# Two-layer mixer encoder on one core: one-time steps inside layer 0, and two projection groups with high and low part in one matmul

## The chip, the cores and the metric

The kernel runs on one core of a Trainium2 chip. The metric is the device time in microseconds (us) of one execution. The kernel before takes 1415.18 us, the median of three runs (1415.05 to 1416.42).

## The reference, cut to what matters

An encoder of two layers works on 256 tokens of width 1024, with a second input `mem` of 256 rows. All values are float32.

```python
for i in range(DEPTH):                       # DEPTH = 2
    h = rms_norm(x, mix_norm_g[i])
    proj = h @ w_in[i]      # attention q, k, v | ssm z | ssm xBC | ssm dt | memory q | gates
    y_da  = diff_attention(q, k, v, lam, ...)                 # 8 heads, alibi slopes
    y_ssm = mamba2_bidir(z, xbc, dt, conv_w, conv_b, ...)     # conv of 5 taps over xbc, chunked scan, both ways
    y_xa  = mem_cross_attention(xa_q, rms_norm(mem, mem_norm_g[i]), w_mem_kv[i])
    merged = g0 * (y_da @ wb_da) + g1 * (y_ssm @ wb_ssm) + g2 * (y_xa @ wb_xa)
    x = x + merged @ w_out[i]
    x = x + swiglu(rms_norm(x, ffn_norm_g[i]))
return rms_norm(x, final_norm_g)
```

`lam` is a scalar of each layer, made from exponentials of four short parameter vectors.

## The kernel before, in words

**High and low parts.** Every large product is made from float32 values split in two: a high part (the value cast to the matmul type fp32r) and a low part (what is left). For a weight W and an activation A the kernel adds W_high x A_high, W_high x A_low and W_low x A_high in PSUM. ScalarE casts the weights (`wH`, L990, `split_h`); VectorE (L1382) or, for some units, GpSimd (L1317) subtracts and writes `wL` (`split_l`).

**Units.** The weights of a layer come as 220 units of 128x1024 floats (512 KB): two K tiles of 128 rows by 512 columns. A ring of four slots holds raw, high and low part. Units are grouped (`layer_groups`); a group of four units fills one of two PSUM pairs (`PS[0]`, `PS[1]`, 1024 columns each), which alternate by the parity of the group. A group of layout T computes the transposed product: in a unit, for each of four column blocks and two K tiles, a matmul of 256 columns with A_high and one with A_low (16), and then eight with W_low: 24 matmuls. Layout N has 12 matmuls of 512 columns. Layout C (most of the FFN) streams `hHL`, where high and low activation lie side by side, as one operand of 512 columns: eight of those and eight of 256 columns; the two halves of the result are added later. C needs twice the PSUM for the same output columns, and takes it from the side banks `S`.

**The order of a layer.** The groups run mk0, mk1, mv0, mv1 (keys and values of `mem`, units 0 to 15), dt (16, 17), xbc4 (18 to 21), xq0 (22 to 25), xbc5 (26 to 29), xq1, xbc0, q0, k0, v0, xbc1, q1, k1, v1 (62 to 65), xbc2, z3, z0 and so on to br, out, ffn and down.

**A plan written out by hand** (`layer_plan`) says after which unit each engine does each side step: `put(u, engine, step, i)`. Each engine walks the units in order (`each_step`): at unit u TensorE does the matmuls of u and then its steps of u; ScalarE does first the cast of unit u+3 and then its steps of u, in the order in which they were put; VectorE does first the subtraction of unit u+3 (where GpSimd does not have it) and then its steps; the SyncE queue issues the load of unit u+3. The cast of u+3 waits until TensorE has used the slot, that is until unit u-1 is done. `pool_splits` gives GpSimd the odd units from 8 on, but none from unit 26 to the gates of branch 1.

**Around units 18 to 28.** TensorE does `dt_turn` after unit 19 and `dt_sums` after unit 25; VectorE does `dt_in` at 20, `dt_u` at 21 (L1660 to L1665), `dt_out` at 23 and the first four conv steps at 22 to 25 (L1646, each four instructions); ScalarE does `dt_exp` at 21, `dt_ln` at 23, and evacuates xbc4 at 22 (L1018 and four of L1022) and xq0 at 26 (L1002). `psum_free` of a pair is raised by whoever evacuated it, and TensorE waits for it at the first unit of the group that uses the pair next.

**The start.** Ahead of unit 0 TensorE transposes `mem` (`mem_turn`, four parts, two of them before unit 0 and two ahead of units 1 and 2), ScalarE scales it and casts units 0 to 2. Then, still ahead of its first planned step, ScalarE squares `mem` (L1043, twice, into row sums), takes the root (L1049), issues the load of x, and takes the exponentials for `lam` (L1263, L1265); VectorE makes the reciprocal, the two diagonal tiles `mdiag` (L1417) and the sums for `lam`. Only after this come the casts of unit 3 and later. `mem_row` on TensorE, after unit 3, broadcasts `mdiag` with two small matmuls. `norm_square` to `norm_scale` (steps 2 to 5) normalise x for `norm_turn` after units 9 to 12. `par_turn` (TensorE, after unit 4) and `params` (VectorE, step 5) bring the parameters (L1398 to L1411).

**The end.** The last `down` group finishes token half 0 before half 1. VectorE adds (L1461) and multiplies by the gain (L1464), ScalarE squares and takes the root (L1279, L1281), and then VectorE (L1823, L1826) and, for the first 512 columns of half 1, ScalarE (L1284) scale; one store for each half follows.

Of the kernel before, what the change touches and what calls it, by code (L numbers as in the profile page):

```python
# [33 lines left out]
ALU = mybir.AluOpType  # L34
AX = mybir.AxisListType

P = 128
# [38 lines left out]
def layer_groups():  # L76
# [11 lines left out]
    return g  # L88


GROUPS = layer_groups()
# [4 lines left out]
assert UNITS % RING == 0 and NGROUPS % 2 == 0  # L96
# [11 lines left out]
def layer_plan():  # L108
# [10 lines left out]
    for g, (kind, b, units, _) in enumerate(GROUPS):  # L119
        if kind == "mk":  # L120
            put(FIRST_UNIT[g] + units + 1, "dve", "mk", g)
        if kind in ("mv", "xq", "q", "k", "v", "xbc", "z", "gate0", "gate1", "gate2"):
# [43 lines left out]
    for h in range(HEADS):  # L166
# [6 lines left out]
        put(u + 4, "pe", "da_turn", h)  # L173
        put(u + 5, "act", "da_copy", h)
        put(u + 6, "pe", "da_values", h)
        put(u + 7, "act", "da_head", h)
# [29 lines left out]
    for i in range(4 * SG):  # L206
# [5 lines left out]
        put(x[i] + 6, "pe", "diag", i)  # L212
# [67 lines left out]
PAR_LOADS, ROW_LOADS = 6, 7  # L280


def build(nc, x, mem, mix_norm_g, w_in, lq1, lk1, lq2, lk2, subln_g, conv_w, conv_b, dt_bias, A_log, D_skip,
# [3 lines left out]
    with ctx:  # L287
# [71 lines left out]
        def conv_tile(n):  # L359
# [12 lines left out]
        sg1 = [sg, scr[:, 0:1024]]  # L372
        hid = scr[:, 0:512]
# [48 lines left out]
            "turned", "h", "ready", "sq", "sum", "std", "diag", "row"))  # L422
        sp_pace, pe_pace = sem("sp_pace"), sem("pe_pace")
# [40 lines left out]
        def unit_source(lay, g, c):  # L464
# [11 lines left out]
            if kind.startswith("br"):  # L476
# [3 lines left out]
                   "gate1": GATE0 + D, "gate2": GATE0 + 2 * D}[kind]  # L480
            return cols(w_in_v, lay, k, col + UC * b)
# [13 lines left out]
        def used_after(lay, g):  # L495

            return lay * (NGROUPS // 2) + g // 2 + 2

        def wait_full(eng, lay, g):

            u = FIRST_UNIT[g] + GROUPS[g][2] - 1
            eng.wait_ge(unit_used[u % RING], use(lay, u) + 2)

        def wait_evacuated(eng, lay, kind, b):
            g = GI[kind, b]
            eng.wait_ge(psum_free[g % 2], used_after(lay, g))
# [26 lines left out]
        def _(sp):  # L533
# [6 lines left out]
            def load(lay, u):  # L540
# [17 lines left out]
                else:  # L558

                    src = unit_source(lay + u // UNITS, g, c)  # L560
                    sp.dma_start(raw[:, slot], src).then_inc(raw_in[slot], 32)
# [57 lines left out]
            sp.dma_start(gB, final_norm_g.partition_broadcast(P)).then_inc(fin_in, 16)  # L619
            sp.wait_ge(fin_second, 1)  # L620
# [5 lines left out]
        def _(pe):  # L626
# [29 lines left out]
            for b in range(2):  # L656
                mem_turn(b)
# [37 lines left out]
            def unit(lay, u, g, c):  # L695
                kind, b, units, layout = GROUPS[g]
                slot, pair = u % RING, g % 2
# [4 lines left out]
                if c == 0 and kind != "outb":  # L702
                    pe.wait_ge(psum_free[pair], lay * (NGROUPS // 2) + g // 2 + 1)
# [3 lines left out]
                if lay == 0 and kind == "mk" and b == 0 and c in (1, 2):  # L707
                    mem_turn(c + 1)
                first_unit, last_unit = c == 0 and kind != "outb", c == units - 1 and kind != "out"
                if layout == "T":  # L710
                    for m in range(4):
                        for kk in range(UT):
# [5 lines left out]
                            mm(o, w_h, aL_[:, k, :], False, False)  # L718
                    pe.wait_ge(l_done[slot], use(lay, u) + 2)
                    for m in range(4):  # L720
                        for kk in range(UT):
                            w_l = wL[:, slot, kk, P * m:P * (m + 1)]
                            ins = mm(dst[:, T * m:T * (m + 1)], w_l, aH_[:, a0 + UT * c + kk, :], False,
                                     last_unit and kk == UT - 1)
                elif layout == "C":
# [245 lines left out]
        def _(act):  # L971
# [21 lines left out]
            def evac(lay, g):  # L993
                kind, b = GROUPS[g][:2]
                pair = g % 2
# [80 lines left out]
            def step(lay, kind, i):  # L1076
                if kind == "evac":
# [26 lines left out]
                elif kind == "hid_corr":  # L1104
                    g = GI["ffn", i]
                    pair = g % 2
# [83 lines left out]
                elif kind == "dt_copy":  # L1190
                    g = GI["dt", 0]
                    wait_full(act, lay, g)
                    nc.scalar.copy(dtT, PS[g % 2][0:64, 0:T]).then_inc(psum_free[g % 2], 1)
# [64 lines left out]
            for t in range(NT):  # L1258
                mem_square(t)
            mem_root()  # L1260
            act.dma_start(xN, x.rearrange("b (t p) d -> p (b t) d", p=P)).then_inc(x_in, 16)
            act.wait_ge(row_in, 16 * ROW_LOADS)
# [588 lines left out]
```

## Time and profile before

| what | value |
|---|---|
| median of three runs | 1415.18 us (1415.05 to 1416.42) |
| the profiled execution, its own time | 1415.59 us |
| its span | 1413.9 us, 22066 instructions |
| TensorE matmul busy | 1393.2 us (99%), 8199 instructions |
| weight loads busy | 1222.2 us (86%) |
| VectorE, ScalarE, GpSimd busy | 923.6 (65%), 884.6 (63%), 322.9 us (23%) |
| DMA | 253.85 MB, mean 180 GB/s |
| mean granted TensorE clock | 0.997 of full speed |

The span runs from the first instruction to the last; the profiled execution's own time is 1.7 us longer than its span and 0.41 us longer than the median. Matmuls are pipelined: what one costs is read from start to start, not from its duration.

### The profile page before, as it was taken

To read this page: it belongs to the slowest core of one execution; us is meant where nothing else is said; L and a number is where in the kernel's file an instruction comes from. 1 tells how busy PE (TensorE), PEld (TensorE's weight loads), DVE (VectorE), ACT (ScalarE), POOL (GpSimd) and SP (SyncE) were. 2 spreads that over 40 slices of the span, in tenths; PEclk is the share of its full clock that TensorE was granted. 3 is DMA by queue.
4 is the path that set the end of the run, shared out by engine and by line. 5 is a ranking of instruction groups with operands and counts; after the bars stand their busy time and mean duration, and the time that the engine had idled before them with its cause. 6 is when DMAs were issued, how large, how long until landed. Compare 5 with 4: busy or idle time off the path is not lost.

```text
span 1413.9 us, 22066 instructions
## 1 busy us (share of the span) xinstructions
PE 1393.2 (99%) x8199; PEld 1222.2 (86%) x8215; DVE 923.6 (65%) x1246; ACT 884.6 (63%) x1428; POOL 322.9 (23%) x161
## 2 busy tenths in 40 slices
PE   6999999999999999999999999999999999999998
PEld 6899898888888889888899998988888888888886
DVE  5567565898998545554453775668989874555532
ACT  6567567886855546555445765878777563555543
POOL 0310000010023444444414000000110244444442
PEclk9999999999999999999999999999999999999999
DMA  7565445566765555656556554465767545566663
GB/s 258 170 195 167 133 135 164 142 194 217 204 189 171 197 179 176 196 181 229 188 184 179 155 163 136 134 179 142 215 200 223 188 165 191 167 192 181 193 193 119
DMA packets 158181, 253.85 MB, mean 180 GB/s; under 512 B 12681, under 2 KB 59899, under 8 KB 157819
## 3 DMA queue, kind: packets, MB, share of 16 engines
q1 hardware_dynamic: 157347, 250.73, 57.6%
q10 hardware_dynamic: 728, 1.71, 0.3%
q8 instruction: 65, 1.06, 0.3%
q14 instruction: 41, 0.34, 0.1%
HBM read 250.18 MB, written 2.23 MB: 179 GB/s over the span
## 4 chain that ended last, share of the span: by engine, by line
PE 88%; DVE 4%; ACT 3%; DVEq 2%; issue 1%; DMA 1%; ACTq 0%; SPq 0%
PE PS L635 71%; PE S L635 14%; DVE wL L1382 1%; ACT wH L990 1%; PE S L642 1%; ACT scr L1148 1%; DMA w_raw<-in_w_in_dram 1%; DVE actLf L1646 1%; PE S L959 0%; PE S L894 0%; DVEq L1717 0%; DVEq L1648 0%; DMA regA<-in_mem_dram 0%; PE S L865 0%; DVE regA L1718 0%
## 5 line engine op out<-in xcount | busy, mean ns | idle before, releaser
L990 ACT CAST wH<-w_raw 128x1024 fp32r<-128x1024 f32 x440 | 457.9, 1043 | 461.0 <-PE PS L635 323.5
L1382 DVE TENSOR_TENSOR wL<-w_raw,wH 128x1024 fp32r<-128x1024 f32 (+1 forms) x328 | 415.5, 1271 | 337.0 <-ACT wH L990 318.4
L1317 POOL TENSOR_TENSOR wL<-w_raw,wH 128x1024 fp32r<-128x1024 f32 (+1 forms) x112 | 270.8, 2418 | 417.3 <-ACT wH L990 417.3
L635 PE MATMUL PS<-hHL,wH 128*128 128x256 f32 (+2 forms) x2016 | 314.8, 303 | 0.0
L635 PEld LDWEIGHTS PS<-hHL,wH 128*128 128x128 f32 (+1 forms) x2016 | 266.4, 190 | 10.9 <-issue 2.6
L635 PE MATMUL PS<-wH,actH 128*128 128x512 f32 x560 | 223.1, 398 | 0.0
L635 PE MATMUL PS<-wH,actL 128*128 128x512 f32 x560 | 218.4, 390 | 0.0
L635 PE MATMUL PS<-wH,hHL 128*128 128x512 f32 x768 | 200.7, 403 | 0.0
L635 PE MATMUL PS<-hHL,wL 128*128 128x256 f32 (+1 forms) x1168 | 172.0, 283 | 0.0
L635 PEld LDWEIGHTS PS<-wH,hHL 128*128 128x128 f32 x768 | 140.1, 188 | 33.2 <-issue 6.5
L635 PEld LDWEIGHTS PS<-hHL,wL 128*128 128x128 f32 (+1 forms) x1168 | 158.4, 190 | 6.2
L635 PE MATMUL PS<-wL,actH 128*128 128x512 f32 x560 | 150.9, 390 | 0.0
L635 PEld LDWEIGHTS PS<-wH,actL 128*128 128x128 f32 x560 | 105.3, 188 | 22.3 <-issue 1.4
L635 PEld LDWEIGHTS PS<-wH,actH 128*128 128x128 f32 x560 | 105.2, 188 | 22.3 <-issue 1.4
L635 PEld LDWEIGHTS PS<-wL,actH 128*128 128x128 f32 x560 | 105.1, 188 | 22.3
L635 PE MATMUL PS<-wL,hHL 128*128 128x512 f32 x384 | 103.2, 390 | 0.0
L635 PE MATMUL S<-hHL,wH 128*128 128x512 f32 x320 | 85.9, 390 | 0.0
L635 PEld LDWEIGHTS PS<-wL,hHL 128*128 128x128 f32 x384 | 72.1, 188 | 15.9
L1344 POOL TENSOR_TENSOR scr<-actHf,dts 128x512 f32<-128x512 f32 x16 | 20.6, 1286 | 271.0 <-PE S L865 207.2
L1333 POOL TENSOR_TENSOR regA<-actHf,dts 128x512 f32<-128x512 f32 x8 | 10.1, 1266 | 269.9 <-ACTq L1189 228.2
L635 PEld LDWEIGHTS S<-hHL,wH 128*128 128x128 f32 x320 | 60.1, 188 | 13.5
L1646 DVE SCALAR_TENSOR_TENSOR actLf<-scr,lp,actLf 128x256 f32<-128x256 f32 x128 | 59.5, 506 | 4.7 <-issue 0.4
(256 smaller groups left out, 1578.3 us busy)
## 6 DMA issues: line engine op xcount, KB each, us to landing
w_raw<-in_w_in_dram SPq DMA_DIRECT2D x192, 512.0 KB
w_raw<-in_w_ffn_in_dram SPq DMA_DIRECT2D x176, 256.0 KB
w_raw<-in_w_branch_dram SPq DMA_DIRECT2D x64, 512.0 KB
w_raw<-in_w_ffn_out_dram SPq DMA_DIRECT2D x44, 512.0 KB
w_raw<-in_w_mem_kv_dram SPq DMA_DIRECT2D x32, 512.0 KB
regA<-cs_rows SPq DMA_DIRECT2D x64, 256.0 KB, 5.2
w_raw<-in_w_out_dram SPq DMA_DIRECT2D x16, 512.0 KB
regA<-in_mem_dram SPq DMA_DIRECT2D x4, 256.0 KB, 5.8
```

The source lines that it names most:

```text
L635: return nc.tensor.matmul(o, l, r, start=first, stop=last, skip_group_check=True)
L642: ins = nc.tensor.transpose(dst[:, at:at + P], src(t, k), ident[:, :])
L990: nc.scalar.copy(wH[:, slot].rearrange("p k c -> p (k c)")[:, q], raw[:, slot].rearrange("p k c -> p (k c)")[:, q]).then_inc(h_done[slot], 1)
L1148: ins = nc.scalar.activation(sc[b][:, T * q:T * (q + 1)], S[q // 2][:, T * (q % 2):T * (q % 2 + 1)], ACT.Exp, bias=nmx[b][:, q:q + 1], sca ...
L1317: nc.gpsimd.tensor_tensor(wL[:, slot].rearrange("p k c -> p (k c)")[:, q], raw[:, slot].rearrange("p k c -> p (k c)")[:, q], wH[:, slot].r ...
L1333: nc.gpsimd.tensor_tensor(v3(xw[i % 2], HPG), v3(xsN[g][:, 1 - c, :], HPG), wgt[:, q:q + HPG].unsqueeze(2).broadcast_to([P, HPG, DH]), ALU ...
L1344: nc.gpsimd.tensor_tensor(v3(xsd[i % 2], HPG), v3(xsN[g][:, c, :], HPG), dgain[:, SH * c + HPG * g:SH * c + HPG * (g + 1)].unsqueeze(2) .b ...
L1382: v.tensor_tensor(wL[:, slot].rearrange("p k c -> p (k c)")[:, q], raw[:, slot].rearrange("p k c -> p (k c)")[:, q], wH[:, slot].rearrange ...
L1646: ins = v.scalar_tensor_tensor(tile[:, j, :], cin[:, j, k:k + T], p_cw[:, q:q + 1], tile[:, j, :], ALU.mult, ALU.add)
```

## The change

1. A new layout W for two groups, xbc4 and xq0. A unit holds four K tiles by 256 columns instead of two by 512; its matmuls stream `hHL` (512 columns) for W_high. Two units fill one PSUM pair (a *fill*), so a W group takes two fills, and the parity of pairs counts fills. Each fill is evacuated by a copy of the low halves on ScalarE (`wide_corr`) and an addition on VectorE (`wide_sum`), which frees the pair. The evacuations of xbc4 (step 22) and xq0 (step 26) on ScalarE go; for xbc4, the middle tap is made from SBUF in `conv_mid`.
2. The squares and root of `mem`, the load of x and the steps for `lam` move from before the first planned step to steps 1 to 6 of layer 0; `params`, and the four steps of the norm of x, move by one to three units. Of the `mem_turn` parts, one is before unit 0 and three lie inside units 0 to 2, after the second column block.
3. Three moves of side steps: `da_turn` to `da_head` of the last head by one unit, the first `cb` from unit 68 to 61, `diag` 11 from unit 108 to 109.
4. At the end each half is scaled right after its root, half by VectorE and half by ScalarE (half 1: 384 columns on ScalarE).

```diff
+WIDE = [("xbc", 4), ("xq", 0)]
+FILLS = [2 if x[3] == "W" else 1 for x in GROUPS]
+FIRST_FILL = [sum(FILLS[:i]) for i in range(NGROUPS)]
+PAIR = [n % 2 for n in FIRST_FILL]
...
+        if (kind, b) in WIDE:
+            for half in range(2):
+                n = 2 * WIDE.index((kind, b)) + half
+                put(FIRST_UNIT[g] + 2 * half + 2, "act", "wide_corr", n)
+                put(FIRST_UNIT[g] + 2 * half + 2, "dve", "wide_sum", n)
+                if kind == "xbc":
+                    put(FIRST_UNIT[g] + 2 * half + 3, "act", "conv_mid", n)
...
-    put(5, "dve", "params")
+    put(7, "dve", "params")
     put(6, "sp", "mem_keep")
+    put(1, "act", "mem_stats")
+    put(2, "dve", "mem_stats")
+    put(4, "dve", "lam_sum")
+    put(5, "act", "lam_exp")
+    put(6, "dve", "lam_out")
     put(3, "pe", "mem_row")
     put(4, "dve", "mem_row")
-    put(2, "act", "norm_square")
-    put(3, "dve", "norm_sum")
-    put(4, "act", "norm_root")
-    put(5, "dve", "norm_scale")
+    put(4, "act", "norm_square")
+    put(5, "dve", "norm_sum")
+    put(6, "act", "norm_root")
+    put(8, "dve", "norm_scale")
...
+        last = h == HEADS - 1
+        put(u + 4 + last, "pe", "da_turn", h)
+        put(u + 5 + last, "act", "da_copy", h)
+        put(u + 6 + last, "pe", "da_values", h)
+        put(u + 7 + last, "act", "da_head", h)
...
-        u = x[4 * g] + (-1, -5, -5, -6)[g]
+        u = x[4 * g] + (-8, -5, -5, -6)[g]
         put(u, "pe", "cb", g)
         put(u + 1, "act", "cb_rows", g)
...
-        put(x[i] + 6, "pe", "diag", i)
+        put(x[i] + (7 if i == 11 else 6), "pe", "diag", i)
...
+                at = col + UC * b + T * (c // 2)
+                return w_in_v[lay, :, 4 * (c % 2):4 * (c % 2) + 4, at:at + T]
...
-            for b in range(2):
-                mem_turn(b)
+            mem_turn(0)
...
-                if c == 0 and kind != "outb":
-                    pe.wait_ge(psum_free[pair], lay * (NGROUPS // 2) + g // 2 + 1)
+                if c == 0 and kind != "outb" or layout == "W" and c == 2:
+                    pe.wait_ge(psum_free[pair], lay * (LAYER_FILLS // 2) + fill // 2 + 1)
...
+                        if lay == 0 and kind == "mk" and b == 0 and c < 3 and m == 1:
+                            mem_turn(c + 1)
...
+                elif layout == "W":
+
+                    at = 4 * (c % 2)
...
+                    for m in range(2):
+                        for kk in range(4):
+                            mm(dst[:, 2 * T * m:2 * T * (m + 1)], w_h[:, kk, P * m:P * (m + 1)], hHL[:, at + kk, :, :],
+                               c % 2 == 0 and kk == 0, False)
+                    pe.wait_ge(l_done[slot], use(lay, u) + 2)
+                    for m in range(2):
+                        for kk in range(4):
+                            ins = mm(dst[:, 2 * T * m:2 * T * m + T], w_l[:, kk, P * m:P * (m + 1)], hH[:, at + kk, :],
+                                     False, c % 2 == 1 and kk == 3)
...
+                if kind == "wide_corr":
+                    g, half = GI[WIDE[i // 2]], i % 2
+                    pair = (PAIR[g] + half) % 2
+                    wait_full(act, lay, g, half)
+                    nc.scalar.copy(v3(corr[pair], 2), halves(PS[pair][:, :])[:, :, 1, :]).then_inc(wide_corr, 1)
+                elif kind == "conv_mid":
+                    b, half = WIDE[i // 2][1], i % 2
+                    act.wait_ge(wide_done, 2 * len(WIDE) * lay + i + 1)
+                    for j in range(2 * half, 2 * half + 2):
...
+                elif kind == "mem_stats":
+                    if lay == 0:
+                        act.dma_start(xN, x.rearrange("b (t p) d -> p (b t) d", p=P)).then_inc(x_in, 16)
+                        for t in range(NT):
+                            mem_square(t)
+                        mem_root()
+                elif kind == "lam_exp":
+                    if lay == 0:
+                        act.wait_ge(row_in, 16 * ROW_LOADS)
+                        nc.scalar.activation(rows3[:, :, 64:128], rows3[:, :, 64:128], ACT.Exp)
+                        act.wait_ge(lam_sum, 1)
+                        nc.scalar.activation(lam4, lam4, ACT.Exp)
+                        act.drain().then_inc(lam_exp, 1)
...
-            act.wait_ge(fin_rstd, NT)
-            nc.scalar.activation(fin[:, 1, 0:UC], fin[:, 1, 0:UC], ACT.Copy, scale=xr[:, 1:2]).then_inc(fin_first, 1)
-            act.wait_ge(fin_first, 1)
+                act.wait_ge(fin_rstd, t + 1)
+                q = slice(UC, D) if t == 0 else slice(0, FIN_ACT)
+                nc.scalar.activation(fin[:, t, q], fin[:, t, q], ACT.Copy, scale=xr[:, t:t + 1]).then_inc(fin_first, 1)
+            act.wait_ge(fin_first, 2)
...
+                    dve.wait_ge(wide_corr, 2 * len(WIDE) * lay + i + 1)
+                    v.tensor_tensor(dst, halves(PS[pair][:, :])[:, :, 0, :], v3(corr[pair], 2), ALU.add
+                                    ).then_inc(psum_free[pair], 1)
+                    dve.drain().then_inc(wide_done, 1)
+                elif kind == "mem_stats":
+                    if lay == 0:
+                        dve.wait_ge(mem_std, 1)
+                        v.reciprocal(mr, mr)
+                        dve.drain()
+                        mem_factors()
...
-                    if i % 4 == 0:
+                    if ("xbc", b) in WIDE:
+                        dve.wait_ge(conv_mid, 2 * lay + i % 4 // 2 + 1)
+                    elif i % 4 == 0:
                         wait_evacuated(dve, lay, "xbc", b)
```

## Rows read from the trace of the kernel before

**Rows 1.** Page, part 4: the chain that ended last, by engine

```profile
PE 88%; DVE 4%; ACT 3%; DVEq 2%; issue 1%; DMA 1%; ACTq 0%; SPq 0%
```

**Rows 2.** Waits of TensorE: who for whom, us in total, times, longest

```profile
PE PS L635 <- ACT wH L990: 5.1, 1, 5.1
...
PE S L865 <- DVEq L1623: 0.8, 2, 0.4
PE S L635 <- ACT scr L1148: 0.7, 2, 0.4
```

**Rows 3.** Timeline, TensorE: start, duration; units 24 and 25 (T), dt_sums, unit 26

```profile
86.20 2.08 PE L635 MATMUL PS<-hHL,wH 128*128 128x256 f32 x16
...
89.08 2.08 PE L635 MATMUL PS<-hHL,wH 128*128 128x256 f32 x16
...
91.96 0.20 PE L635 MATMUL S<-aH,upR 128*128 128x64 f32 x1
...
92.58 2.13 PE L635 MATMUL PS<-hHL,wH 128*128 128x256 f32 x16
```

**Rows 4.** Timeline, TensorE, the first matmuls of two units of layout C

```profile
569.21 1.09 PE L635 MATMUL PS<-hHL,wH 128*128 128x512 f32 x4
...
572.00 1.09 PE L635 MATMUL PS<-hHL,wH 128*128 128x512 f32 x4
```

**Rows 5.** The chain in order of time: start, us; all of unit 3

```profile
24.75 5.11 PE PS L635 x24
```

**Rows 6.** Timeline, ScalarE and VectorE, the steps ahead of the first planned one

```profile
17.51 1.06 ACT L1043 ACTIVATE regA<-regA 128x1024 f32<-128x1024 f32 x1
...
21.04 0.30 ACT L1049 ACTIVATE small<-small 128x2 f32<-128x2 f32 x1
...
21.62 0.48 DVE L1417 TENSOR_SCALAR regB<-ident,small 128x128 f32<-128x128 f32 x2
...
23.56 2.94 ACT L990 CAST wH<-w_raw 128x1024 fp32r<-128x1024 f32 x3
```

**Rows 7.** Timeline, TensorE, the first matmul of unit 5

```profile
33.26 0.36 PE L635 MATMUL PS<-actH,wH 128*128 128x256 f32 x1
```

**Rows 8.** DMA view of 0 to 40 us, one figure per us

```profile
GB/s 0 21 215 236 207 236 367 393 401 379 371 371 265 151 87 33 18 162 344 410 408 307 393 385 184 25 18 207 309 322 193 303 420 449 401 367 367 340 326 209
```

**Rows 9.** Windows: stretch, busy times of the engines, granted TensorE clock, DMA

```profile
24.70:27.00 2.30, 2.25 (x10) 2.28 (x11) 2.30 (x3) 1.82 (x3) 0.00 (x0) 0.50 0.06 24
```

**Rows 10.** Timeline, ScalarE, VectorE and GpSimd, steps 21 to 24 of layer 0

```profile
80.18 0.31 ACT L1197 ACTIVATE scr<-scr 128x128 f32<-128x128 f32 x1
...
82.56 1.93 ACT L1022 ACTIVATE regA<-PS,lp 128x256 f32<-128x256 f32 x4
...
82.10 2.27 DVE L1665 TENSOR_TENSOR scr<-scr,dts 128x128 f32<-128x128 f32 x1
...
91.10 1.23 DVE L1382 TENSOR_TENSOR wL<-w_raw,wH 128x1024 fp32r<-128x1024 f32 x1
92.24 1.83 DVE L1646 SCALAR_TENSOR_TENSOR regA<-scr,lp,regA 128x256 f32<-128x256 f32 x4
...
81.82 2.40 POOL L1317 TENSOR_TENSOR wL<-w_raw,wH 128x1024 fp32r<-128x1024 f32 x1 [3.82 <-ACT wH L990]
```

**Rows 11.** Groups of 560 to 640 us: xcount, busy us, mean ns, idle before

```profile
L1108 ACT COPY scr<-PS 128x512 f32<-128x512 f32 x7 | 4.1, 580 | 0.0
...
L1550 DVE TENSOR_TENSOR scr<-PS,scr 128x512 f32<-128x512 f32 x7 | 4.8, 692 | 13.5 <-ACT scr L1109 13.5
```

**Rows 12.** Timeline, TensorE, end of unit 108 and diag 11

```profile
390.33 1.07 PE L635 MATMUL PS<-wL,hHL 128*128 128x512 f32 x4
391.71 1.10 PE L635 MATMUL S<-actHf,regA 128*128 128x64 f32 x8 [0.31 <-DVEq L1728]
```

**Rows 13.** Timeline, the end: VectorE scales half 0; the last store is issued

```profile
1408.73 0.75 DVE L1826 TENSOR_SCALAR regB<-regB,small 128x1024 f32<-128x1024 f32 x1
...
1410.37 0.35 ACTq L1287 DMA_DIRECT2D out_dram<-regB  x1
```

More of the change, by code:

```diff
@@ L87, in layer_groups @@
     g += [("down", nb, FT // UT, "N") for nb in range(2)]
-    return g
+    return [(kind, b, n, "W" if (kind, b) in WIDE else layout) for kind, b, n, layout in g]
+WIDE = [("xbc", 4), ("xq", 0)]
 GROUPS = layer_groups()
@@ L493, in past_end, with used_after, wait_full @@
             return lay == DEPTH - 1 and u >= UNITS
[L495 to L501, printed above, removed]
+        def used_after(lay, fill):
+            return lay * (LAYER_FILLS // 2) + fill // 2 + 2
+        def wait_full(eng, lay, g, half=1):
+            u = FIRST_UNIT[g] + (GROUPS[g][2] - 1 if half else 1)
             eng.wait_ge(unit_used[u % RING], use(lay, u) + 2)
@@ L505, in wait_evacuated @@
             g = GI[kind, b]
-            eng.wait_ge(psum_free[g % 2], used_after(lay, g))
+            fill = FIRST_FILL[g] + FILLS[g] - 1
+            eng.wait_ge(psum_free[fill % 2], used_after(lay, fill))
         def each_step(engine, unit_fn, evac_fn, step_fn):
@@ L696, in unit @@
                 kind, b, units, layout = GROUPS[g]
-                slot, pair = u % RING, g % 2
+                fill = FIRST_FILL[g] + (c // 2 if layout == "W" else 0)
+                slot, pair = u % RING, fill % 2
                 if kind == "ffn" and b in (1, 2) and c == 0:
@@ L1192, in step @@
                     wait_full(act, lay, g)
[L1193 removed]
+                    nc.scalar.copy(dtT, PS[PAIR[g]][0:64, 0:T]).then_inc(psum_free[PAIR[g]], 1)
                     act.drain().then_inc(dt_copied, 1)
@@ L1493, in step @@
                     params(lay)
+                elif kind == "wide_sum":
+                    (what, b), half = WIDE[i // 2], i % 2
+                    g = GI[what, b]
+                    pair = (PAIR[g] + half) % 2
+                    q = slice(2 * half, 2 * half + 2)
+                    if what == "xq":
+                        if lay == 0 and b == 0:
+                            dve.wait_ge(mem_stored, 16)
+                        dst = xqT[:, 4 * b:4 * b + 4, :][:, q]
+                    else:
+                        dst = cin[:, q, 2:2 + T]
+                    dve.wait_ge(wide_corr, 2 * len(WIDE) * lay + i + 1)
[8 more added lines that the diff above has]
+                        mem_factors()
+                elif kind == "lam_sum":
+                    if lay == 0:
+                        dve.wait_ge(row_in, 16 * ROW_LOADS)
+                        lam = scr[:, 2048:2560].rearrange("p (a q c) -> p a q c", a=2, q=2)
+                        v.tensor_tensor(v3(scr[:, 4096:4352], 2), lam[:, :, 0, :], lam[:, :, 1, :], ALU.mult)
+                        dve.drain()
+                        v.tensor_reduce(lam4, scr[:, 4096:4352].rearrange("p (a c) -> p a c", a=4), AX.X, ALU.add)
+                        dve.drain().then_inc(lam_sum, 1)
+                elif kind == "lam_out":
+                    if lay == 0:
+                        v.memset(cin[:, :, 0:2], 0.0)
+                        v.memset(cin[:, :, 2 + T:4 + T], 0.0)
+                        dve.wait_ge(lam_exp, 1)
+                        v.tensor_tensor(nlam2, lam4[:, 2:4], lam4[:, 0:2], ALU.subtract)
+                        dve.drain()
+                        for n in range(DEPTH):
+                            v.tensor_scalar(nlam2[:, n:n + 1], nlam2[:, n:n + 1], -lambda_init(n), None, ALU.add)
+                        dve.drain()
                 elif kind == "norm_sum":
```

86 lines of the change are left out of this document (34 added, 52 removed).

## The prediction

> **What bounds the kernel now.** The chain that ended last comes first: 88% of it is TensorE [rows 1], so apart from the start and the end only two things count, the distance of matmuls from start to start and the waits of TensorE. The waits view lists nearly all of the second kind: one of 5.1 us in the start, and five short ones in the body, of which two pairs are shown [rows 2] and the fifth is 0.31 us [rows 12]. The timeline gives the first kind: a unit of layout T takes 89.08 - 86.20 = 2.88 us [rows 3], one of layout C, with the same products, 572.00 - 569.21 = 2.79 us [rows 4]. VectorE and ScalarE are 65% and 63% busy over the span, but this mean says little: around unit 24 VectorE has no idle time at all, and that is where the change gives it more work.
>
> **Layout W, what it saves.** W has the matmuls of C (eight of 512 columns, eight of 256). The saving is 2.88 - 2.79 = 0.09 us a unit, for 8 units in each of two layers: 0.7 us a layer, 1.4 us in all. From below it could be nothing; more than this no row supports. Its loads are rows of 1 KB where T has 2 KB; the FFN loads have 1 KB too and layout C still goes at its pace, so I count nothing; were a load late, the ring of four slots (some 8 us) covers it.
>
> **Layout W, what it adds.** Per fill, ScalarE gets a copy of 128x512 (0.58 us) and VectorE an addition of 128x512 (0.69 us), both read from the same pair of operations in the FFN [rows 11]. ScalarE loses two copies of 128x1024 for four of these and comes out even. VectorE gets four additions, 2.8 us a layer, and the pair is now freed by the last of a chain: matmuls, copy, addition. Behind each addition, on VectorE's queue, stand the conv step and the later `split_l`; in front of it stands all that VectorE is late with. So each must be walked. With TensorE 0.09 us a unit quicker, unit 24 would start at 85.66 and unit 26 at 91.86 (now 92.58 [rows 3], less 8 x 0.09).
> - `wide_sum` 0 (step 20): VectorE is idle there; nothing waits.
> - Step 21: ScalarE now does `conv_mid` 0 (half of the 1.93 us of four activations) ahead of `dt_exp`. It begins 0.3 us earlier, so `dt_exp` ends at 81.1 instead of 80.49 [rows 10]. `dt_u` follows; its multiplication, a 128x128 operation, took 2.27 us, since it ended with GpSimd's subtraction (81.82 + 2.40 = 84.22; the multiplication ended at 84.37 [rows 10]). The same collision comes 0.4 us later: GpSimd to 84.6, `dt_u` to 84.75.
> - `wide_sum` 1 (step 22): 84.85 to 85.55. It frees the pair of unit 24 (85.66): just in time, 0 to 0.4 us late. I take 0.
> - `conv` 0: 85.6 to 87.5; `split_l` 26 to 88.65; `dt_out` (1.6) to 90.3; `conv` 1 (1.9) to 92.2. Now the same point is 91.10 [rows 10].
> - Step 24: `split_l` 27 (1.14 from 91.10 to 92.24 [rows 10]) to 93.3, and only then `wide_sum` 2 to 94.0. It frees the pair that xbc5, unit 26, needs at 91.86. TensorE waits 2.15 us. Even without any delay in the steps before, 91.10 + 1.14 + 0.69 = 92.93 would be 1.1 us late.
> - `wide_sum` 3 (step 26) ends near 101; its pair is wanted by unit 30, near 106. Nothing.
>
> A small SBUF operation that finishes with GpSimd's, as in rows 10, is also what a page describes. The Trainium skill, SBUF — State Buffer, "SBUF: two separate sides", says that VectorE's operations with two SBUF inputs and GpSimd's take one pair of ports whole, one after the other. By that rule `wide_sum`, with one input in PSUM, is never held up. The trace agrees: in the FFN the like addition takes 692 ns in the mean, although GpSimd subtracts there too [rows 11].
>
> So W costs 2.15 - 0.70 = +1.45 us a layer, **+2.9 us** in both; ends: -1.4 (no wait) and +4.0 (2.7 us of wait).
>
> **The start.** TensorE waits 5.1 us before unit 3, from 19.6 to 24.75, because ScalarE reaches the cast of unit 3 only at 23.56 [rows 6], and unit 3 then takes 5.11 us [rows 5] instead of 2.88: the granted clock is 0.50 there [rows 9], 1.2 GHz. Unit 5 starts at 33.26 [rows 7]. After the change the cast of unit 3 comes at once, and unit 3 runs at full clock from about 20.1 to 23.0 (the later `mem_turn` parts cost ScalarE 1.3 us, which this leaves out of no sum, since a later wait hides it). But `mem_row` stays after unit 3 and needs `mdiag`, and this moved:
> - ScalarE, step 1: the cast of unit 4 must have its load. The loads of 4 and 5 were issued at 12; little moved from 14 to 17 [rows 8]; about 0.9 MB had come by 20. Estimate: cast from 20.1 to 21.2.
> - The load of x issues here, behind that wait, 1 us or so later than now; `norm_square` wants it at 28, when it lands.
> - Squares, table load, root: 17.51 to 21.34, 3.83 us [rows 6], now to 25.0.
> - Step 2: the cast of unit 5 (2.94 / 3 = 0.98 [rows 6]) to 26.0; VectorE subtracts (1.2) to 27.25, and only then makes reciprocal and tiles (0.8, as from 21.34 to 22.10 [rows 6]): 28.1.
>
> TensorE stands from 23.0 to 28.15: 5.1 us again. The wait has only changed its name. Unit 4 starts at 28.6. After an idle time of the same length I take the same half clock: 5.1 to 5.2 us, then `par_turn`, and unit 5 at 34.15: **+0.9 us**. Ends: -1.5 if the clock stays up, +2 if it comes back a unit later or if the next point fails. Steps 4 to 8 on VectorE: `params` and `norm_scale` (8) end near 47.9 by my walk, with one more wait for GpSimd; `norm_turn` after unit 9 comes at 48.1. Cover: 0.2 us. `lam` itself has room to unit 48.
>
> The Trainium skill, TensorE: Matmul & The Clock Gate, "What's actually happening", says that the monitor of the clock runs freely, so that the moment of a change differs from run to run. By that rule the same gap may in some executions cost no half clock, and the start would come out at -1.5. The one trace shown has a single gap of this length and it did fall, and the three runs lie within 1.4 us, so this is a rival and not the forecast.
>
> **Three moved steps.** `da_turn` of head 7 and the first `cb` wait in both layers (waits of 0.8 and 0.7 in all [rows 2]), `diag` 11 in layer 0 (0.31 [rows 12]): 1.8 us. From start to start they cost more: the last matmul before `diag` 11 starts at 390.33 + 3 x 0.227 = 391.01, the next would be due at 391.24, and it starts at 391.71: 0.47 us. The other four, read so, are 0.52 to 0.57; sum 2.65, and with the unit behind it 2.7. Ends: 0 (each finds a wait in its new place) and -2.8. At 61 bank 0 has been free since `da_exp` 59, and `xs_turn` in it comes a unit later; `da_turn` 7 has a whole unit for what was 0.4 us late; bank 2 is wanted again only at 81. I take **-2.7 us**.
>
> **The end.** Now VectorE scales all of half 0 from 1408.73 to 1409.48 [rows 13], and the reciprocal of half 1 stands behind it. Half 0 would be done before half 1 arrives (delay of half 1: 0.1 us at most), the reciprocal comes 0.5 us earlier, and the last store issues at 1409.9 instead of 1410.37 [rows 13]. The two stores, now 0.9 us apart, no longer share the DMA engines; I add 0.5 us for that, a guess from the 3.5 us from that issue to the end. **-1.0 us**; ends -0.3 and -1.4.
>
> **Sum:** +2.9 + 0.9 - 2.7 - 1.0 = +0.1 us on 1415.59, which is 1415.7; the median of the runs is 0.41 lower, so 1415.3. This measurement can tell about 0.2%, 2.8 us, from no change.
>
> **Rivals.**
> - *VectorE keeps up* and TensorE does not wait at unit 26. For it: if the multiplication in `dt_u` gets in before GpSimd, the walk is 1.7 us shorter and the wait 0.4. Against: now, without any addition, VectorE is already too late by 1.1. W then gives -1.4, the total is -4.2: 1411. Chance 0.22. With the next one besides, 1408.7: 0.05.
> - *The clock stays up* over the gap before `mem_row`: -2.3, total -2.2, 1413. 0.16.
> - *Slower:* the clock falls in the new gaps ahead of unit 26. It needs 2.2 us of idle to be enough; then unit 26 costs 2.2 us more (5.11 against 2.88), twice: 1415.3 + 4.4 = 1419.7. Against: no gap in the body shown is that long, and in the start it took 5.1. 0.08.
> - *VectorE is late for `norm_turn`*, by a further subtraction of GpSimd (2.4), or moved steps wait again: +2 to +3, 1417.5 to 1418.5. 0.09.
> - That the change does not do what it says is part of the forecast: the start is not shortened.
>
> **Numbers.** The forecast's own case has 0.40, and its own range is 1413.5 to 1417.3. The range of 8 in 10 takes in most of *keeps up* and of *late for norm_turn*: 1410.4 to 1418.5. Faster: 0.22 + 0.05 and 0.06 from the low ends of the others, 0.33. Slower: 0.08, half of 0.09, and 0.06 for a wait that I don't see, 0.19. Within: 0.48.
>
> **What would show it.** Waits of TensorE: `psum_free` from the new addition ahead of unit 26, near 2 us in both layers (right), or none (the first rival); a wait of `mem_row` near 5 us in place of that before unit 3, and the granted clock of unit 4; none left for L865, the first `cb` and `diag` 11; W units at 2.79 us; the last store some 3.4 us before the end. If unit 5 starts before 32.5, my start is wrong; if xbc5 starts within 0.7 us of xq0's end and `dt_sums`, my walk of VectorE is.

## The result, and the profile after

| | median, us | executions | lowest to highest |
|---|---|---|---|
| before, beside it | 1415.47 | 12 | 1413.89 to 1416.42 |
| after | 1419.38 | 12 | 1416.83 to 1421.12 |

The ratio is 1.0026, with a 95% interval of 1.0019 to 1.0033: slower by 3.9 us. The forecast was 1415.3 with a range up to 1418.5; the measured median lies 4.1 us above the first and 0.9 us above the second. The profiled execution of after took 1420.75 us, its span is 1419.0 against 1413.9: 5.1 us more.

The waits of TensorE (for whom, us in total, times, longest) answer to [rows 2]:

```profile
PE S L663 <- DVEq L1479: 4.4, 1, 4.4
PE PS L663 <- DVE regA L1576: 4.1, 2, 2.1
PE PS L663 <- ACT wH L1032: 3.0, 1, 3.0
...
PE S L907 <- DVEq L1732: 0.3, 1, 0.3
```

The first is the wait of `mem_row`, in place of the 5.1 us before unit 3. The second is new: twice 2.07 us, ahead of unit 26 in each layer, released by `wide_sum` 2 (L1576 adds). The third lies ahead of unit 0, at 7.70 us, where TensorE waits for the first cast; the trace before waits there for loads of `mem` instead (1.25 and 2.17 us). The waits of `da_turn` 7, `cb` 0 and `diag` 11 are gone. So far this is the forecast. The last row isn't: it is a wait of 0.26 us for VectorE ahead of `da_turn` 4 in layer 1 (949.33 us), where the trace before has none. The chain by engine has changed too [rows 1]:

```profile
PE 95%; DVE 2%; ACT 1%; DVEq 1%; issue 1%; DMA 0%; SPq 0%; ACTq 0%
```

This share can't tell where the time went: it is 95% too in the trace of a1 below, whose span is 8.0 us shorter, and 85% in that of c1, 3.4 us shorter. The starts of units can. The timeline of TensorE around unit 26 of layer 0 (start, duration) answers to [rows 3]:

```profile
81.51 2.00 PE L663 MATMUL PS<-hHL,wH 128*128 128x512 f32 x8
...
84.30 2.00 PE L663 MATMUL PS<-hHL,wH 128*128 128x512 f32 x8
...
89.93 2.00 PE L663 MATMUL PS<-hHL,wH 128*128 128x512 f32 x8
...
93.23 0.28 PE L663 MATMUL S<-aL,onesR 128*128 128x128 f32 x1
95.57 3.68 PE L663 MATMUL PS<-hHL,wH 128*128 128x256 f32 x16 [2.07 <-DVE regA L1576]
...
100.04 2.08 PE L663 MATMUL PS<-hHL,wH 128*128 128x256 f32 x16
```

A unit of W takes 84.30 - 81.51 = 2.79 us, as layout C does. The 16 matmuls of unit 26, behind the wait, take 3.68 us where those of unit 27 take 2.08; the unit as a whole takes 100.04 - 95.57 = 4.47 us instead of some 2.9. The windows say why (the last columns: granted clock, share of the DMA engines, GB/s):

```profile
93.30:95.50 2.20, 0.20 (x2) 0.06 (x1) 2.13 (x3) 1.21 (x2) 0.00 (x0) 1.00 0.05 20
95.50:97.00 1.50, 1.43 (x7) 1.43 (x8) 1.29 (x4) 0.00 (x0) 0.00 (x0) 0.56 0.57 66
97.00:98.00 1.00, 1.00 (x6) 1.00 (x6) 0.92 (x3) 0.00 (x0) 0.00 (x0) 0.50 0.94 365
98.00:99.00 1.00, 1.00 (x6) 1.00 (x6) 1.00 (x2) 0.00 (x0) 0.00 (x0) 0.50 0.17 61
99.00:100.00 1.00, 1.00 (x10) 1.00 (x9) 0.93 (x3) 0.00 (x0) 0.00 (x0) 0.95 0.18 14
```

The clock is 1.00 while TensorE stands, and falls to 0.50 (1.2 GHz) as unit 26 begins: 6 matmuls a us instead of 10 or 11. It is back near 99.1. Layer 1 shows the same, with the same 2.07 us of wait:

```profile
789.52 0.28 PE L663 MATMUL S<-aL,onesR 128*128 128x128 f32 x1
791.86 1.55 PE L663 MATMUL PS<-hHL,wH 128*128 128x256 f32 x6 [2.07 <-DVE regA L1576]
```

One such fall, 3.4 us at half the clock (here from about 95.7 to 99.1), lowers the mean clock of an execution by 3.4 x 0.5 / 1419 = 0.0012 (an estimate from these rows), so two make it 0.994 where it would be 0.997. Not every execution falls so. The mean clock of the twelve, beside their times:

```
0.994:  1419.36 1419.39 1419.43 1419.90 1420.72 1420.75 1421.12
0.996:  1417.18 1418.93
0.997:  1416.83 1417.26 1417.49
```

Seven have 0.994, as two falls give; the four lowest are near 1417, at 0.996 and 0.997; the one of 1418.93 could have one fall. Only one execution has a full trace here; that the low ones kept the clock at unit 26 is read from these two columns alone. The trace of a1, which has no gap at unit 26, has 0.996 too, so 0.996 doesn't tell one fall from none. The experiment d1 below shows by itself that the loss hangs on the idle time.

VectorE's queue shows why `wide_sum` 2 is late. Steps 21 to 24 of layer 0, which answer to the VectorE rows of [rows 10]:

```profile
84.25 1.95 DVE L1776 TENSOR_TENSOR scr<-scr,dts 128x128 f32<-128x128 f32 x1
86.28 0.69 DVE L1576 TENSOR_TENSOR scr<-PS,scr 128x512 f32<-128x512 f32 x1
87.12 1.83 DVE L1757 SCALAR_TENSOR_TENSOR regA<-scr,lp,regA 128x256 f32<-128x256 f32 x4
...
91.79 1.83 DVE L1757 SCALAR_TENSOR_TENSOR regA<-scr,lp,regA 128x256 f32<-128x256 f32 x4
93.69 1.23 DVE L1443 TENSOR_TENSOR wL<-w_raw,wH 128x1024 fp32r<-128x1024 f32 x1
94.83 0.68 DVE L1576 TENSOR_TENSOR regA<-PS,scr 128x512 f32<-128x512 f32 x1
```

The addition of 0.68 us is done at 95.51. In the queue it stands behind conv 1 (91.79) and the subtraction for unit 27 (93.69), which nobody waits for yet.

The start, on TensorE: end of unit 3, `mem_row`, unit 4, unit 5.

```profile
22.89 1.12 PE L663 MATMUL PS<-actH,wL 128*128 128x256 f32 x8
28.43 1.19 PE L663 MATMUL S<-regB,onesR 128*128 128x128 f32 x4 [4.43 <-DVEq L1479]
29.28 0.56 PE L663 MATMUL PS<-actH,wH 128*128 128x256 f32 x1
...
34.66 0.36 PE L663 MATMUL PS<-actH,wH 128*128 128x256 f32 x1
```

Unit 4 takes 5.38 us, nearly all of it at half clock, and unit 5 comes 1.40 us later than in [rows 7]. Not all of this comes from the wait: unit 0 took 6.10 us here (7.70 to 13.80) and 5.17 before (8.01 to 13.18). The end: half 0 stored early, half 1 last.

```profile
1413.33 0.36 SPq L649 DMA_DIRECT2D out_dram<-regB  x1
...
1415.94 0.35 ACTq L1348 DMA_DIRECT2D out_dram<-regB  x1
```

The last issue lies 3.06 us before the end of the span; before it was 1413.9 - 1410.37 = 3.53 us [rows 13].

The bookkeeping of the two profiled executions, by the starts of units: start +1.4; W -0.55 in each layer; wait +2.14 in each (89.08 to 92.58 before, 89.93 to 95.57 now); half clock +1.54 in each; moved steps about -1.2 in layer 0 and -0.35 in layer 1; end -1.0. Sum 1.4 - 1.1 + 4.3 + 3.1 - 1.6 - 1.0 = +5.1. The -0.35 holds a loss of 0.37 at `da_turn` 4, the row of 0.3 above. The waits views of all six kernels below with layout W on show it, and none with W off does, so it belongs to W.

### The profile page after: what moved, and what is told of

It reads as the page before. It is cut to its first block, busy times and chain, and to the rows that moved or that the text cites. A ratio compares the mean times of both kernels' runs of the same rounds, so it can differ in the third digit from the quotient of the medians.

```text
span 1419.0 us, 21836 instructions
## 1 busy us (share of the span) xinstructions
PE 1396.9 (98%) x8071; PEld 1219.8 (86%) x8087; DVE 928.5 (65%) x1254; ACT 884.8 (62%) x1433; POOL 322.8 (23%) x161
## 3 DMA queue, kind: packets, MB, share of 16 engines
q10 hardware_dynamic: 728, 1.71, 0.3%
## 4 chain that ended last, share of the span: by engine, by line
PE 95%; DVE 2%; ACT 1%; DVEq 1%; issue 1%; DMA 0%; SPq 0%; ACTq 0%
PE PS L663 76%; PE S L663 16%; PE S L670 1%; PE S L907 1%; PE S L936 1%; PE S L1001 1%; ACT wH L1032 0%; DVE wL L1443 0%; DMA w_raw<-in_w_mem_kv_dram 0%; DVE regA L1757 0%; DVE scr L1776 0%; PE S L876 0%; PE S L927 0%; DVEq L1759 0%; DVEq L1578 0%
## 5 line engine op out<-in xcount | busy, mean ns | idle before, releaser
L663 PEld LDWEIGHTS PS<-hHL,wH 128*128 128x128 f32 (+1 forms) x1888 | 260.2, 192 | 19.4 <-DVE regA L1576 4.4
L1757 DVE SCALAR_TENSOR_TENSOR actLf<-scr,lp,actLf 128x256 f32<-128x256 f32 x128 | 56.3, 481 | 5.0 <-issue 0.9
```

Source lines behind the costliest of these rows:

```text
L663: return nc.tensor.matmul(o, l, r, start=first, stop=last, skip_group_check=True)
L1757: ins = v.scalar_tensor_tensor(tile[:, j, :], cin[:, j, k:k + T], p_cw[:, q:q + 1], tile[:, j, :], ALU.mult, ALU.add)
```

## The experiments

Each kernel was measured beside the kernel before on the same chip. Its medians there were 1415.20 us (a1 to a4), 1415.22 (b4, b1, c1, c2) and 1414.94 (d1, b3). Unless it is said otherwise a kernel is the one after with the edit shown, and "after" and "before" are the two kernels of this document. Beside the kernel after it was 1415.47, so a time set straight against 1419.38 holds up to 0.5 us of difference between chips; each ratio is taken against the kernel before beside it and free of this. Brackets hold its 95% interval.

**a1: layout W off.**

```diff
-WIDE = [("xbc", 4), ("xq", 0)]
+WIDE = []
```

> The changed kernel with both W groups back in layout T; start, moved steps and end as changed. Theory (the wait for wide_sum 2 ahead of unit 26, and the half clock after it, make the change slow): both waits of 2.1 us go, and the clock stays up at unit 26. Start +1.4, moved steps -1.6, end -1.0 remain: 1.2 us faster than before, within 0.5 us of that in every execution, and no second drop of the clock. Rival (the start is what costs, and W is near neutral): 3 to 4 us slower than before, as the changed kernel is.

Measured: 1413.15 us (1412.73 to 1414.94, 11 executions), ratio 0.9988 [0.9979, 0.9996]. No wait ahead of unit 26 and no fall of the clock there. Layout W costs 1419.38 - 1413.15 = 6.2 us (6.0 if each is taken against the kernel before beside it), and the rest of the change gains 2.05, more than the 1.2 expected. By the starts of units between this trace and that of after, W costs -0.54 + 2.14 + 1.54 around unit 26 in each layer, 6.3 us.

**a2: the conv steps of xbc4 two units later.**

```diff
-            put(u + q, "dve", "conv", 4 * n + q)
+            put(u + q + (2 if b == 4 else 0), "dve", "conv", 4 * n + q)
```

> The changed kernel with the four conv steps of xbc4 on VectorE two units later (24 to 27), so that wide_sum 2 is not behind two of them. Theory (VectorE's queue order is the cause): wide_sum 2 ends near 93.4, at the time at which unit 26 is due; the wait shrinks from 2.1 us to under 0.3 us in both layers, unit 26 runs at full clock, W then saves its 0.09 us a unit: 2.3 us faster than before, and 5 to 7 us faster than an execution of the changed kernel with two drops. Rival (the addition's place in the chain copy, addition, free is too late in itself): a wait of 1 us or more stays, and the time is near 1415.

Measured: 1415.98 us (1414.85 to 1417.89), ratio 1.0005 [0.9996, 1.0014]. The wait at unit 26 is gone and the clock stays up there, 3.4 us less than after. The expectation was 2.3 us faster than before, and it is not faster. But a part of the wait only moved: ScalarE now stands for the last conv step before `conv_silu` 0, with the casts queued behind it:

```profile
104.76 1.06 ACT L1251 ACTIVATE regA<-regA 128x1024 f32<-128x1024 f32 x1 [4.47 <-DVEq L1759]
```

and TensorE then waits twice in each layer, 0.8 us ahead of unit 34 and 0.6 us right behind it, which costs 0.97 and 0.89 us from start to start (its waits view; the longest in the first row is that ahead of unit 0):

```profile
PE PS L663 <- ACT wH L1032: 4.2, 3, 2.6
...
PE S L663 <- ACT regA L1044: 1.1, 2, 0.6
```

**a3: mem_row two units later**, so that TensorE works on through units 4 and 5; VectorE evacuates mk0 after it, and `norm_turn` to `norm_low` move by two.

```diff
-    put(3, "pe", "mem_row")
-    put(4, "dve", "mem_row")
+    put(5, "pe", "mem_row")
+    put(6, "dve", "mem_row")
+    put(6, "dve", "mk", 0)
...
-        put(9 + b, "pe", "norm_turn", b)
+        put(11 + b, "pe", "norm_turn", b)
```

> The changed kernel with mem_row two units later (after unit 5), mk0's evacuation behind it at step 6, and norm_turn and its followers two units later. Theory (mem_row's wait for mdiag holds TensorE in the start): the 4.4 us wait goes, unit 4 runs at full clock, unit 5 starts near 27.5 instead of 34.7, and if nothing later waits the kernel is 7 us faster than the changed one; a wait of VectorE's chain for the norm may give back up to 3 us. Rival (the casts of units 4 to 7, whose loads land late, are the bound): unit 5 starts after 31, and at most 3 us are gained.

Measured: 1415.21 us (1414.32 to 1417.37), ratio 1.0001 [0.9992, 1.001]. That is 4.2 us less than after. Unit 5 starts at 25.97, 7.3 us earlier than in [rows 7], but 4.2 of them are given back by unit 18, most of it in waits of 1.51 and 1.71 us ahead of units 8 and 12, where the keys are evacuated late:

```profile
PE PS L664 <- DVE regA L1577: 4.2, 2, 2.1
PE PS L664 <- DVE actHf L1693: 3.2, 2, 1.7
```

At unit 18 it is 3.1 us ahead. Both gaps ahead of unit 26 are there (2.08 us of wait each), and here the clock fell behind one of them only, in layer 1. It did not fall behind the waits of 1.51 and 1.71 us. Its windows:

```profile
786.00:787.00 1.00, 0.47 (x2) 0.47 (x3) 0.86 (x2) 0.00 (x0) 0.00 (x0) 0.77 0.07 8
787.00:788.00 1.00, 1.00 (x7) 1.00 (x7) 0.93 (x4) 0.00 (x0) 0.00 (x0) 0.50 0.61 137
```

Unit 26 took 2.97 us in layer 0 and 4.48 us in layer 1: the same kernel, the same gap, one fall.

**a4: the edits of a2 and a3 together.**

> Both edits before this together. Theory: they add up, since one acts before 45 us and the other at unit 26 of each layer: 1415.5 - 2.3 - 7 = about 1406 to 1409, and the clock falls nowhere in the body. Rival (the slack won in the start is lost in the norm steps): 1410 to 1413.

Measured: 1412.82 us (1411.55 to 1413.89), ratio 0.9984 [0.9975, 0.9993]. The expected 1406 to 1409 did not come; its rival, 1410 to 1413, did. The mean clock is 0.998 to 1.0 in all executions. What is left is the waits that both edits made: 1.07 and 1.55 us ahead of units 8 and 12, and 0.81 and 0.56 us around unit 34 in each layer.

**b4: the kernel before, with the three moved steps alone** (change 3 of the list).

> The kernel before with nothing but the three moved steps (last head, first cb, diag 11). Theory from the first experiment's trace: 1.0 us less in layer 0 and 0.9 in layer 1, so 1.9 us faster than before, and 0.8 us short of the 2.7 that the prediction summed from the waits. Rival (the prediction's sum): 2.7 us faster.

Measured: 1413.36 us (1412.44 to 1415.81), ratio 0.9987 [0.9978, 0.9996]: -1.9 us. The theory had -1.9. In its trace the moves give -1.31 us in layer 0 and -0.72 in layer 1. `diag` 11 is what differs: -0.48 in layer 0, where there was a wait to remove, and +0.23 in layer 1, where there was none.

**b1: W and the three moves undone**, so that start and end alone are left.

> The changed kernel with T for both W groups and with the three steps back in their old places: what stays is the start and the end. Theory: start 0 to +1.4 (its wait has moved from unit 3 to mem_row), end -1.0: between 1 us faster than before and 0.4 slower, median near 1415. Rival (the start gains after all, as it is meant to): 2 us or more faster.

Measured: 1414.58 us (1413.6 to 1416.33), ratio 0.9997 [0.9988, 1.0005]: -0.6 us, not separated from zero. In its trace unit 5 starts 0.36 us later than before, and in that of a1 0.05 later; in that of after it was 1.40. With an end of -1.0 the start is worth about +0.4 in the median, with an interval of some 1.2 us either way.

**c1: the addition ahead of the subtraction in step 24.**

```diff
+                    if u == FIRST_UNIT[GI["xq", 0]] + 2:
+                        step(lay, "wide_sum", 2)
                     split_l(lay, u + LOOKAHEAD)
```

> The changed kernel with wide_sum 2 ahead of split_l 27 on VectorE instead of behind it. It comes 1.14 us earlier, so the wait ahead of unit 26 shrinks from 2.1 to about 1.0 us, not to nothing. Theory (it is the length of TensorE's idle time that costs the clock, and 1 us is not enough): no drop of the clock in the body in any execution, 2.2 us less from the waits, and the spread of the changed kernel's times (1416.8 to 1421.1) closes at its lower end: 1415 to 1416. Rival (any idle time behind the small matmuls of dt_sums can cost the clock): drops still happen, in fewer or as many executions, with times up to 1419.

Measured: 1416.16 us (1414.69 to 1418.57), ratio 1.0005 [0.9996, 1.0014], 3.2 us less than after (3.0 if each is taken against the kernel before beside it). VectorE and TensorE in its trace:

```profile
94.16 0.69 DVE L1577 TENSOR_TENSOR regA<-PS,scr 128x512 f32<-128x512 f32 x1
94.99 1.23 DVE L1444 TENSOR_TENSOR wL<-w_raw,wH 128x1024 fp32r<-128x1024 f32 x1
```

```profile
94.91 2.17 PE L664 MATMUL PS<-hHL,wH 128*128 128x256 f32 x16 [1.02 <-DVE regA L1577]
```

The wait is halved, to 1.02 us, and the clock stays up in this trace in both layers. The mean clock is 0.997 in ten executions and 0.996 in the slowest, 1418.57, so none has two falls, and one fall in that one is not excluded. VectorE is still late: TensorE waits 0.34 us for it ahead of `cs_turn`, behind unit 28, and that unit is 0.5 us longer than in after. The median is a little above the 1415 to 1416 expected. So half the wait is worth more than half the loss.

**d1: the gap filled.** `dt_sums`, just ahead of the gap, makes its last two products nine times instead of once, with the same result.

```diff
-                    mm(S[0][:, P:2 * P], onesR[:, :], aH_t[:, :], True, False)
-                    mm(S[0][:, P:2 * P], onesR[:, :], aL_t[:, :], False, True).then_inc(cs_done, 1)
+                    for again in range(9):
+                        mm(S[0][:, P:2 * P], onesR[:, :], aH_t[:, :], True, False)
+                        ins = mm(S[0][:, P:2 * P], onesR[:, :], aL_t[:, :], False, True)
+                    ins.then_inc(cs_done, 1)
```

> The kernel after the change, but the two last matmuls of dt_sums (128 columns) are repeated eight times more, with the same result, in the time in which TensorE stands ahead of unit 26. wide_sum 2 comes as late as before, so the matmuls of unit 26 start at the same time; what changes is only that the time in front is not idle. Theory (the half clock of unit 26 comes from the idle time, and is a cost apart from the wait): no clock of 0.5 at unit 26 in either layer, unit 26 back at 2.9 to 3.0 us from 4.47, 3.1 us less than the executions that fell: 1416.5 to 1417.3, and no execution above 1418.5. Rival (the first matmuls on a pair freed late are slow for another reason, such as the traffic around them, or the drop comes from small matmuls being too little work): unit 26 stays at 4.4 us and the time at 1419.4, or more.

Measured: 1417.58 us (1416.15 to 1418.71), ratio 1.0017 [1.0008, 1.0026]. The last copy and unit 26 in its trace, and its windows there:

```profile
94.48 0.27 PE L663 MATMUL S<-aL,onesR 128*128 128x128 f32 x1
95.06 2.18 PE L663 MATMUL PS<-hHL,wH 128*128 128x256 f32 x16 [0.31 <-DVE regA L1578]
```

```profile
95.50:97.00 1.50, 1.50 (x15) 1.50 (x14) 1.41 (x4) 0.00 (x0) 0.00 (x0) 1.00 0.89 218
97.00:98.00 1.00, 1.00 (x11) 1.00 (x10) 0.94 (x1) 0.00 (x0) 0.00 (x0) 1.00 0.51 197
```

Unit 5 was 0.52 us earlier here, and unit 26 starts 0.51 us earlier: the addition comes no sooner, counted from there. Yet the 16 matmuls take 2.18 us instead of 3.68, and unit 26 is 1.50 us shorter in both layers. No execution has a mean clock under 0.996, against 0.994 in seven of twelve before the edit. The median is 1.8 us below that of after, but 1.3 when each is taken against the kernel before beside it, and the two ratios' intervals overlap. The spans are clearer: their median is 1415.1 us, and 1417.6 in after. An execution's own time is 1.7 to 3.1 us longer than its span here, and 1.7 to 1.8 in all other kernels; why is open, and it may be what puts the median and the slowest execution 0.3 and 0.2 us above what the theory had. What shows the cause is unit 26 itself: the addition comes as late as before, only the idle time is gone, and the half clock with it. The other reading (a slow unit for another reason) falls.

**c2: the start of a3, the addition of c1, and a milder form of a2** (conv 1 to 3 of xbc4 and `conv_silu` 0 one unit later).

```diff
-            put(u + q, "dve", "conv", 4 * n + q)
-        put(u + {4: 6, 5: 5, 0: 3, 1: 5, 2: 6, 3: 6}[b], "act", "conv_silu", n)
+            put(u + q + (1 if b == 4 and q else 0), "dve", "conv", 4 * n + q)
+        put(u + {4: 7, 5: 5, 0: 3, 1: 5, 2: 6, 3: 6}[b], "act", "conv_silu", n)
```

> W kept, with VectorE's queue mended: wide_sum 2 ahead of split_l 27, conv steps 1 to 3 of xbc4 one later, conv_silu 0 one later; and the later mem_row of the earlier experiment. Theory: no wait ahead of unit 26, and none handed on to xbc0 (there ScalarE stood 4.5 us in conv_silu and was late with its casts); W then gives its 1.3 us: 1.5 to 2.5 us faster than a4_both, near 1410.5, the fastest so far. Rival (VectorE has no room for four more additions, wherever they stand): another wait of 1 us or more appears between units 26 and 36, near 1412.5.

Measured: 1408.87 us (1407.78 to 1409.94, 5 executions), ratio 0.9951 [0.9938, 0.9963]: faster than both kernels by 6.3 and 10.5 us. The waits at unit 26 and around unit 34 are gone. These are its longest apart from one for a load at the very start: the first row is 1.02 and 1.71 us ahead of units 8 and 12, the second the wait ahead of unit 0.

```profile
PE PS L665 <- DVE actHf L1694: 2.7, 2, 1.7
PE PS L665 <- ACT wH L1034: 2.7, 1, 2.7
```

**b3: c2 without W** (`WIDE = []`, and conv as in after).

> The version that beat both kernels (mem_row later, the addition first in its step) with layout W switched off and the conv steps where the change has them: what W itself is worth when nothing waits for its additions. Theory (W saves 0.55 to 0.7 us a layer at its own units and its additions cost nothing once they are in time): 1.1 to 1.4 us above 1408.9, so 1410.0 to 1410.3. Rival (the additions still push other work of VectorE back, so that W brings nothing even then): 1408.9 or less.

Measured: 1409.72 us (1408.94 to 1410.17, 5 executions), ratio 0.996 [0.9947, 0.9972]. That is 0.85 us above c2, less than the 1.1 to 1.4 expected, and the two ratios' intervals overlap, so the medians alone don't separate them. The unit starts say the same size: c2 gains 0.64 us over b3 between units 18 and 88 of layer 0, and 0.29 in the same stretch of layer 1, where W brings a loss of 0.35 ahead of `da_turn` 4, behind unit 67. From unit 18 to the end of the last unit it is 1.45 us.

The trace of b3 shows one thing more. Its mk0 is evacuated late as in a3, TensorE waits 1.95 us ahead of unit 8, and the clock falls behind it:

```profile
36.90 0.50 PE L664 MATMUL PS<-wH,actH 128*128 128x512 f32 x1 [1.95 <-DVE actHf L1693]
```

```profile
36.90:37.90 1.00, 1.00 (x4) 0.86 (x5) 1.00 (x1) 0.99 (x2) 1.00 (x1) 1.00 0.93 356
38.50:41.00 2.50, 2.50 (x8) 1.94 (x7) 1.90 (x4) 1.56 (x2) 1.40 (x2) 0.50 0.21 66
```

Unit 8 takes 4.44 us there and 2.86 in c2. So half the clock behind a wait is not special to unit 26. This execution has a mean clock of 0.998 and is b3's slowest; its other four have 0.999 or 1.0, so they will have kept the clock, and the median is not touched.

## Why the prediction was wrong, point by point

**The step that failed** is that behind the wait at unit 26 TensorE goes on at full clock. The forecast had the gap right: "TensorE waits 2.15 us", measured 2.14. What the gap does to the clock was the slower rival, with a chance of 0.08, because "no gap in the body shown is that long, and in the start it took 5.1". That the trace of before shows no gap of 2 us in its body is no evidence on what one does. After its first 8 us it has no wait between 0.41 and 5.1 us, so it was open over that whole stretch whether the clock falls; a chance near a half would have been fairer. The fall cost 1.54 us a unit, not the 2.2 that the rival had (the clock was back before the end of the unit), 3.1 in both layers. That is three quarters of the 4.1 us between forecast and result. It brings the forecast to 1418.4, just inside the range; the moved steps, which gave 0.8 us less than forecast, take it past the end.

The Trainium skill, TensorE: Matmul & The Clock Gate, "What's actually happening", says that the monitor of the clock runs freely. The prediction drew on this for the start alone; by the same rule a gap at unit 26 would fall in some executions and not in others. The trace agrees: a3 has two equal gaps and one fall, and seven executions of after have the mean clock of two falls while three have that of none.

**Layout W, what it saves**: 0.09 us a unit, as forecast (2.79 us each); 0.55 a layer by the trace instead of 0.70. **What it adds**: the walk of VectorE held, with the collision with GpSimd (the multiplication took 1.95 us at 84.25), `wide_sum` 1 just in time (done at 86.97, unit 24 starts at 87.09), and the sub-step order that puts the addition behind `split_l` 27. Everything came 1.4 us later than in the walk because the start did, TensorE's wish for the pair as well, so the wait was the same. The term was +2.9 and W measures +6.0 to +6.2: 3.1 from the clock, about 0.2 from a smaller saving.

**The start**: "The wait has only changed its name" held: 5.1 us were forecast between unit 3 and `mem_row`, and it was a wait of 4.43 us with 1.2 GHz behind it. Unit 3 started at 20.90, not 20.1. By the start of unit 5 it came out between -0.09 (a2) and +1.77 us (c1) in the six traces with this start, +0.4 by b1 and the end, for a forecast of +0.9. Most of this spread lies in two units that run at half pace, wholly or in part (0.21 us from start to start of 256 columns instead of 0.12): unit 0 takes 5.16 us in a1, 6.10 in after and 6.05 in c1, and unit 4 takes 4.85, 5.38 and 5.35, so it is a matter of when the clock comes back. The start of before moves as well: in b4, which has the same start, unit 5 begins 0.68 us earlier than in [rows 7]. *The clock stays up* did not come about in any trace that has this gap. It does in a3 and c2, but there the gap itself is gone. `norm_scale` took 3.33 us (45.05 to 48.38) where it took 1.42 before; a subtraction of GpSimd ran from 44.76 to 47.17. `norm_turn` did not wait.

**Three moved steps**: -2.7 forecast, -1.9 by b4. The sum counted what leaves the old place and nothing in the new one. `diag` 11 was moved in both layers and had a wait in one; `da_turn` and `cb` gave 0.83 and 0.95 us in the two layers, where 1.1 was read from starts. The trace of after keeps one wait of this line (L907) that was to be gone, that of `da_turn` 4.

**The end**: -1.0, as forecast, in the traces of after and of b1.

The terms as the runs have them: W +6.2, start +0.4, moves -1.9, end -1.0, sum +3.7; measured +3.9. All but the end are differences of medians, good to about 1.2 us each, so that the sum comes so close is in part luck. That the start was 0.5 us better than forecast hid a part of what the moved steps lacked. The rivals *VectorE keeps up* and *late for norm_turn* did not happen.

What isn't settled is how long a wait can be without a fall, and how often it then falls. In the traces, after the first 8 us, the clock stays up behind waits of 0.94 and 1.02 (c1), 1.07 and 1.55 (a4), 1.51 and 1.71 (a3) and 1.02 and 1.71 us (c2). It falls behind 1.95 (b3) and behind three of the four of 2.07 and 2.08 us (after, a3). Each is a single execution, no run was made to vary the length alone, and a3 shows that one gap without a fall proves little.

## What to carry to other kernels

A wait of the bottleneck engine has two prices, its length and what the clock does behind it; a gap of 2 us in the body cost 2.1 us of standing and, in most executions here, 1.5 us more. So cut such a gap in two, or fill it with matmuls, before looking for larger savings, and when a new gap is longer than any in the old trace, give its effect on the clock a real chance. And where an operation frees a buffer that the bottleneck wants, put it ahead of work that only has to be done by the next unit: moving one addition ahead of one subtraction gave some 3 us in the median.

## What the runs showed of the hardware that was not expected

Behind 2.07 us of standing, the granted clock fell to 0.50 at about the moment at which the matmuls began again, and stayed there for 3.4 us. In b3 it fell only 1 us after the matmuls were back, behind 1.95 us of standing: the price of a gap can come when the engine is busy again. After the 4.4 us wait of the start it stayed at 0.50 for nearly the whole of unit 4. The same gap in one execution fell in layer 1 and not in layer 0 (a3). With the gap filled by 128-column matmuls up to 0.31 us it did not fall in either layer of the trace (d1), and neither behind 1.02 us (c1); none of the 22 executions of these two kernels has the mean clock of two falls. Two groups of times of one kernel on one core, 1416.8 to 1417.5 and 1419.4 to 1421.1 with one execution between, can thus come largely from the clock behind a single pair of gaps.
